# The projections of the HGRN2 heads, the pooling input and the branch gates by Strassen's seven block products

## What is computed

```python
h = rmsnorm(x, gains[2])
z = h @ w_in                       # 1024 x (4*1024 + 512 + 2*1024)
q, fz, iv, og, u, ga, gb = split(z)
k = (1 - lb) * sigmoid(-fz); logf = log(1 - k)
o, s_new = hgrn_chunked(silu(q), k, iv, logf, state)   # 8 heads, chunks of 64
o = o * rsqrt(mean(o * o) + EPS) * a_gnorm
y_a = (o * silu(og)) @ w_a_up
y_b = (scale * groupwise_linear(trailing_mean_w(u) - u)) @ w_b_up   # w = 2, 4, 8, 16
m = sigmoid(ga) * y_a + sigmoid(gb) * y_b
x = x + rmsnorm(m @ w_out, gains[3])
```

## Time and profile before

| | |
|---|---|
| time, median of 3 runs | 2529.26 us (2527.71 to 2529.55) |
| the profiled execution's own time | 2532.01 us |
| its span, first to last instruction | 2530.2 us |
| granted TensorE clock, mean | 0.982 |
| matmuls | 21376 |
| busy share: PE, PEld, DVE, ACT, POOL | 95%, 81%, 51%, 42%, 36% |

### The profile page before, as it was taken

How to read it: one execution, slowest core, us unless ns; L and a number is a source line. 1 busy time by engine, 2 the same in 40 slices (tenths; PEclk the granted TensorE clock), 3 DMA queues, 4 the chain that set the end, 5 groups by cost and what they waited for, 6 DMA issues and landing times.

```text
span 2530.2 us, 54119 instructions
## 1 busy us (share of the span) xinstructions
PE 2401.1 (95%) x21376; PEld 2056.4 (81%) x21376; DVE 1301.3 (51%) x2188; ACT 1060.0 (42%) x1913; POOL 904.3 (36%) x713
## 2 busy tenths in 40 slices
PE   6899999999999999999999999988999999999888
PEld 5688888888888777777878888877888888888776
DVE  7766666300366666666682212268666666000845
ACT  6433333333454444444442332555333334334565
POOL 2577776422212111111221221302777776222110
PEclk9999999999999999999999999999999999999999
DMA  3111112412121011111201112321121112321201
GB/s 124 42 58 50 50 58 63 130 47 68 60 81 37 26 36 36 36 28 36 70 16 38 50 46 87 115 77 35 50 58 55 53 50 79 115 67 48 63 18 69
DMA packets 98195, 147.22 MB, mean 58 GB/s; under 512 B 10160, under 2 KB 43184, under 8 KB 98096
## 3 DMA queue, kind: packets, MB, share of 16 engines
q1 hardware_dynamic: 70352, 121.14, 16.0%
q10 hardware_dynamic: 27744, 24.68, 3.0%
HBM read 131.70 MB, written 14.09 MB: 58 GB/s over the span
## 4 chain that ended last, share of the span: by engine, by line
PE 67%; DVE 21%; issue 8%; ACT 2%; DVEq 1%; POOL 1%; DMA 0%; ACTq 0%; POOLq 0%; SPq 0%
PE bank L687 15%; PE bank L688 15%; PE bank L689 15%; PE bank L718 6%; PE bank L721 6%; PE bank L720 6%; DVE hid L1652 3%; DVE work L1650 3%; DVE hid L1768 2%; DVE hid L1498 1%; PE bank L800 1%; PE bank L833 1%; PE bank L813 1%; DVE ops L1504 1%; DVE hid L1595 1%
## 5 line engine op out<-in xcount | busy, mean ns | idle before, releaser
L597 POOL TENSOR_TENSOR ring<-wtmp,ring 128x512 f16<-128x512 f32 x269 | 339.1, 1263 | 1268.4 <-ACT ring L957 1266.6
L718 PE MATMUL bank<-ops,ring 128*128 128x264 f16 x2240 | 621.2, 277 | 31.5 <-DVE work L1622 22.6
L687 PE MATMUL bank<-ops,ring 128*128 128x264 f16 x2176 | 609.3, 280 | 40.8 <-DVE hid L1689 24.6
L720 PE MATMUL bank<-ops,ring 128*128 128x264 f16 x2240 | 620.8, 277 | 0.0
L721 PE MATMUL bank<-ops,ring 128*128 128x264 f16 x2240 | 620.8, 277 | 0.0
L688 PE MATMUL bank<-ops,ring 128*128 128x264 f16 x2176 | 609.0, 280 | 0.0
L689 PE MATMUL bank<-ops,ring 128*128 128x264 f16 x2176 | 608.6, 280 | 0.0
L687 PE MATMUL bank<-hid,ring 128*128 128x264 f16 x2124 | 589.6, 278 | 1.7 <-DVE hid L2001 1.7
L688 PE MATMUL bank<-hid,ring 128*128 128x264 f16 x2124 | 589.5, 278 | 0.0
L689 PE MATMUL bank<-hid,ring 128*128 128x264 f16 x2124 | 589.4, 278 | 0.0
L610 POOL TENSOR_TENSOR ring<-ring 128x512 f16<-128x512 f32 x240 | 295.1, 1250 | 94.3 <-ACT ring L1008 94.3
(11 more groups left out here) (160 smaller groups left out, 2862.3 us busy)
## 6 DMA issues: line engine op xcount, KB each, us to landing
ring<-weights SPq DMA_DIRECT2D x429, 256.0 KB, 2.7
hid<-xT SPq DMA_DIRECT2D x8, 528.0 KB, 8.3
hid<-out_x ACTq DMA_DIRECT2D x4, 1056.0 KB, 10.9
out_x<-hid ACTq DMA_DIRECT2D x4, 1056.0 KB, 5.4
ops<-xT ACTq DMA_DIRECT2D x3, 1056.0 KB, 9.4
out_x<-ops ACTq DMA_DIRECT2D x3, 1056.0 KB, 5.0
ops<-out_x ACTq DMA_DIRECT2D x3, 1056.0 KB, 8.1
out_x<-ops SPq DMA_DIRECT2D x12, 264.0 KB, 2.2
```

What stands on the lines that cost most here:

```text
L597: nc.gpsimd.tensor_tensor(low(slot), wtmp[:, u % 2, :], high(slot), ALU.subtract).then_inc(unit_ready, 1)
L687: nc.tensor.matmul(out, whi, rhs(t, k, g, 0), start=(k == 0), stop=False)
L718: nc.tensor.matmul(out, whi, xhi, start=(kk == 0 and k != JOINED), stop=False, skip_group_check=True)
L720: nc.tensor.matmul(out, whi, xlo, start=False, stop=False, skip_group_check=True)
```

## The change

The stage `heads` becomes 16 pairs, two per head turn: first q with og, then f with V, and u's four columns at the end in the order w = 16, 8, 4, 2. The gates become eight pairs, one for each m, and beside them runs the plain stage `outs` (up_A and up_B, three units a turn, banks 4 to 7); the pooling's group products are a stage `pools`. These pairs are "chained": they have only banks 0 to 3. Product 2 is added onto product 0 in the same bank, product 4 onto that, product 5 onto that, product 6 onto product 3; ACT copies the bank out after products 0, 2 and 4, and the next product waits for that copy. VectorE adds copy and bank for three of the four blocks, ACT reads the fourth (product 5) itself.

The core of the diff (lines that only pass on new arguments are left out):

```diff
-    "heads": dict(units=8, turns=HEADS, ks=[KD] * 4, kinds="M" * HEADS, banks=4),
-    "gates0": dict(units=8, turns=1, ks=[KD, KD, 1, 1, 1, 1, KD, 4], kinds="M", banks=BANKS),
-    "gates": dict(units=7, turns=7, ks=[KD, KD, KD, 4], kinds="M" * 7, banks=BANKS),
+    "heads": dict(pairs=2 * HEADS, chained=True),
+    "pools": dict(units=1, turns=1, ks=[1] * 4, kinds="M", banks=4, bank0=4),
+    "gates": dict(pairs=KD, chained=True),
+    "outs": dict(units=3, turns=KD, ks=[KD, 4], kinds="M" * KD, banks=4, bank0=4),
...
+CHAIN_BANKS = ((0, 1), (2, 3), (0, 1), (2, 3), (0, 1), (0, 1), (2, 3))
+CHAIN_FRESH = (0, 1, 3)
...
                     with sp.Fori(1, s["pairs"]) as p:
                         load_pair(name, p)
+                        for n in beside:
+                            for u in range(units_of(n)):
+                                load(n, p, u, plan.freed_by(n, p - 1, u))
...
             def head_hooks(h):
                 hh = h - 1
+                return [{
+                    (0, 1): [lambda: keys_and_values(h), lambda: head_transposes(hh, "vT", V)],
+                    (3, 1): [lambda: operands(hh, 1), lambda: head_transposes(hh, "kT", W[3])],
+                    (4, 1): [lambda: operands(hh, 3), lambda: head_scores(hh, "L32", W[0], W[0])],
+                    (6, 1): [lambda: operands(hh, 5), lambda: head_scores(hh, "L16", W[1], W[1]),
+                             lambda: operands(hh, 7), lambda: head_scores(hh, "D16", W[4], W[2])],
+                }, {
+                    (0, 1): [lambda: head_updates(hh, range(4))],
+                    (1, 1): [lambda: head_updates(hh, [4])],
+                    (4, 1): [lambda: operands(hh, 8), lambda: head_outputs(hh)],
+                    (5, 1): [lambda: head_sumsq(hh)],
+                }]
```

The order of ACT in a head turn after the change (p0, p1 are the turn's two pairs; `ahead` takes the high halves for the next turn's first pair):

```diff
+                logf(hh)
+                state_load(hh)
+                chain_copies("heads", p0, 0)
+                if with_norm:
+                    onorm(h - 2, W[4])
+                scale("heads", p1)
+                exps_32(hh)
+                chain_copies("heads", p0, 2)
+                exps_16(hh)
+                to_high("heads", p1, (0, 1), freed0)
+                chain_copies("heads", p0, 4)
+                exps_decay(hh)
+                to_high("heads", p1, (2, 3), freed0)
...
+                    to_high("heads", p1, (4,), freed0)
+                    act.wait_ge(operand_ready, hh * 8 + 8)
...
+                    nc.scalar.activation(Q[:, 0:T], V[:, 0:T], ACT.Silu).then_inc(q_ready, 1)
...
+                    nc.scalar.activation(og, og, ACT.Silu).then_inc(og_ready, 1)
+                    to_high("heads", p1, (5, 6), freed0)
+                chain_copies("heads", p1, 0)
...
+                    scale("heads", h * 2)
...
+                chain_copies("heads", p1, 2)
+                ahead(0, 1)
+                chain_copies("heads", p1, 4)
                 state_store(hh)
+                if not u_turn:
+                    nc.scalar.preload_act_table_set("sigmoid_and_others")
+                ahead(2, 3)
+                osquares(hh)
...
+                    for e in range(2):
+                        b = chained("heads", p1, 5, e)
+                        nc.scalar.activation(gcols(K_, 2 * e + 1), bank[b][:, 0:N], ACT.Sigmoid, scale=-1.0 / WS)\
+                            .then_inc(bank_read[b], 1)
+                    ln_exp_tables()
+                ahead(4, 5, 6)
```

VectorE's order in the same turn (the lines with a minus stood there before; waits left out):

```diff
-                evac_tok(hh, "vT", vtok)
-                if with_norm:
-                    onorm(h - 2)
                 dve.wait_ge(logf_ready, hh + 1)
                 V_.tensor_tensor_scan(GG, smask, W[2], 0.0, ALU.mult, ALU.add).then_inc(cum_ready, 1)
...
+                evac_tok(hh, "vT", vtok)
                 minus_ref(W[0], 64, 31)
+                sums_a("heads", p0, a0)
+                if with_norm:
+                    onorm(h - 2, W[5], W[4])
                 minus_ref(W[1], 32, 15)
                 minus_ref(W[2], 16, 7)
                 operand(W[3], K_, hh, 1)
...
                 evac_scores(hh, "L16", 1)
                 evac_scores(hh, "D16", 2)
+                sums_a("heads", p1, a1)
...
                 V_.tensor_copy(mark[:, 1:2], mark[:, 0:1]).then_inc(chain_ready, 1)
                 if u_turn:
-                    pooling(0)
-                    pooling(1)
+                    pooling(POOL_ORDER[0], p0, 1, 5)
+                    sums_b_odd("heads", p1, b1)
+                    pooling(POOL_ORDER[1], p0, 3, 6)
```

`onorm` loses its product with silu(og): the outputs are multiplied with it when they are read from their banks, and ACT squares them there in four parts. A gate turn of ACT after the change:

```diff
+                def gate_turn(m, dst_a, dst_b, last=False):
+                    prep("outs", m, 0, 1, 2)
...
+                    if not last:
+                        scale("gates", m + 1)
+                    chain_copies("gates", m, 0)
+                    ahead(0, 1)
+                    chain_copies("gates", m, 2)
+                    ahead(2, 3)
+                    chain_copies("gates", m, 4)
+                    ahead(4)
```

Between the first head and the others VectorE and ACT now also make the input sums for the tokens (VectorE's order):

```diff
-            for g in range(1, G):
-                head0_silus(g)
+            t_block(1, (1, 2))
+            head0_silus(1)
+            t_lows(1, 2)
+            t_block(1, (3,))
+            head0_silus(2)
+            t_lows(1, 3, 1)
+            t_block(1, (4,))
+            head0_silus(3)
+            t_lows(1, 4)
             dve.wait_ge(lb_ready, 1)
             decay_keys(0)
```

More of the change, by code:

```diff
@@ L59 @@
 UPS = [("ffn1_up0", "ffn1_up"), ("ffn2_up0", "ffn2_up")]
+BESIDE = {"outs": "gates"}
 PRODUCTS = 7
@@ L176, in __init__ @@
-            for b in range(s["banks"]):
-                uses[b] += self.per(name, b) * s["turns"]
-            unit += s["units"] * s["turns"]
-            ready += s["units"] * s["turns"]
-            plain += s["units"] * s["turns"]
-            used += len(mid_units(name)) * s["turns"]
-            for u in range(s["units"]):
-                loads[self.slot(name, u)] += s["turns"]
-            first = (first + s["units"]) % RING
+            if name in BESIDE:
+                continue
+            group = [name] + [n for n in ORDER if BESIDE.get(n) == name]
@@ L185, in __init__ @@
+            unit += unit_step * (turns - 1)
+            ready += ready_step * (turns - 1)
             if name == "heads":
@@ L665, in take, with turn @@
                     pe.wait_ge(bank_read[b], uses)
-            def turn(name, i, kind, rhs, ready=None, hooks=None):
+            def turn(name, i, kind, rhs, ready=None, hooks=None, order=None):
                 s = STAGES[name]
@@ new lines, in chain_copies, with sums_read @@
+            def chain_copies(name, p, k):
+                for e in range(2):
+                    b = chained(name, p, k, e)
+                    nc.scalar.activation(chain_copy(k, e), bank[b][:, 0:N], ACT.Copy, scale=1.0 / WS)\
+                        .then_inc(bank_read[b], 1)
+            def sums_read(name, p, *ks):
+                for k in ks:
+                    for e in range(2):
+                        b, uses = plan.product(name, p, k, e)
+                        act.wait_ge(bank_read[b], uses + 1)
```

828 lines of the change are left out of this document (484 added, 344 removed).

## The result

The changed kernel takes 2568.13 us (median of 4 runs, 2566.65 to 2570.49) against 2529.41 us for the kernel before (4 runs): a ratio of 1.0155, interval 1.0137 to 1.0172. Slower was forecast, and 2557.4 us.

The account below looks back on a forecast made before the run. TensorE, busy 95% of the span, was taken as the bound. Saving -65.0, steady head turns +43.8, entry +18, last head turn +22.6, into the gates -1.5, gate turns +10.2: +28.1, so 2557.4 us; range 2508 to 2592.

Parts of the forecast that it names:

- kT: Keys' transpose in a head turn: TensorE waits for VectorE's first operand, 23.2 us of chain against 16.4, a 6.9 us hole.
- P4: Last key update, behind product 1 of the second pair: TensorE waits 3.3 us for VectorE's state chain.
- The clock: Behind a hole TensorE's granted clock falls to its lower level: 1.7 to 3.0 us on top, taken as 2.0.
- Entry: Separate first head and turn 1: VectorE's differences and low halves cause waits of 3.6 and about 4 us; net +18.
- Last head turn: Two poolings precede the reading of the output banks, beside the steady turns' waits; net +22.6 us.
- SS: Sums of squares in the last head turn: TensorE waits for output banks behind two poolings, 7.4 us (6.7 to 9.5).
- Into the gates: Turn from the last head into the gates: old waits of 5.8 us and more replaced by smaller ones, net -1.5.
- Gate turns: Product 2 of a gate pair waits 1.7 us for ACT's copy of product 0, six turns, +10.2.
- A: Faster: no hole at the keys' transpose in turns 2 to 8, 7 x 8.9 us less, 2495 us; chance 0.17.
- B: Slower: gate loads queue, a hole of 4 us with its clock, +4.3 in 7 turns, 2587 us; chance 0.13.
- C: VectorE and GpSimd slow each other in the chain before the keys' transpose, 2.3 us x 7, 2574 us; chance 0.12.
- D: Nearly nothing: half of the forecast holes come, 2529 us; chance 0.08.

Follow-up runs that it names:

- experiment 9: The changed kernel with the last key update behind product 3, the head norm behind the third operand, all gate copies first: 2501.92 us, ratio 0.9882.
- experiment 1: The changed kernel with the last key update moved from behind product 1 to behind product 3 of the second pair: 2535.51 us, ratio 1.0007.
- experiment 2: The changed kernel with VectorE's norm of the head before moved from ahead of the first operand to behind the third: 2550.66 us, ratio 1.0057.
- experiment 5: The changed kernel with VectorE's group 1 silus before the first differences and the key decay before the last low halves: 2572.69 us, ratio 1.0146.
- experiment 4: The changed kernel with ACT's gate copies first and high halves 2 to 6 behind the sigmoids: 2549.92, 2549.96 and 2557.13 us, ratio 1.0083.
- experiment 6: The changed kernel with GpSimd's low halves in the head pairs cut to 16 of 512 columns: 2558.00 us, ratio 1.0100.
- experiment 10: experiment 9 with VectorE's sums of product 1, first operand and copies of the keys' transpose made earlier in a head turn: 2511.86 us, ratio 0.9919.
- experiment 12: experiment 10 with D16 scores and key updates one product later, ACT's copy of product 4 first, VectorE's L32 copies and even sums earlier: 2501.68 us.

## Why the prediction was right, by its own steps

**The saving**: right, 576 matmuls; the accounts of both spans close with it.

**Steady turns.** kT: 23.2 us of chain against 16.4 of cover was forecast, 6.9 of hole (the two give 6.8). The changed kernel stands 1.67 at product 3 and 5.01 at kT, together 6.7. ACT's part took 7.1 (898.6 to 905.72) and not 8.0, VectorE's 15.7 (to kT's start at 921.46) and not 15.2, with a stretch by GpSimd of 1.1 in it (2.99 and 1.85 for 2.42 and 1.29). So 22.8 for 23.2, and the cover was 16.1. P4: 3.4 against 3.3, at the place named. The clock: 2.0 a hole was a little dear. In the seven periods TensorE is busy for 410.9 us, and in experiment 9, at full speed, for 387.7 with the same matmuls: 23.2 us for seven holes at kT and seven at P4, 1.7 each. That these holes are the cause, and not the extra work as such, is shown by experiments 1 and 2. The whole was some 7 us too dear over seven periods.

**Table load.** It takes 1.28 us and the next function starts 0.02 us behind it (899.02 to 900.32), as in the earlier trace rows. The drain of 1.38 us that the Trainium skill (ScalarE: Activation LUTs, What ACT_TABLE_LOAD costs) adds is not seen here either.

**Entry.** Holes of 5.8 and 6.3 for the 3.6 and 4 forecast, 1.1 and 3.3 for the 2 and 3.3. The two first were mis-sized: the eight differences took 7.0 us for four where 5.0 stood in the sum, as GpSimd made its first sums beside them. But these are not waits that an order makes, as the sum has them ("stand ahead of"): by experiment 5 VectorE's amount of work is the bound.

**Last head turn: the term that was mis-sized.** The hole at SS was put at 7.4 us, between 6.7 and 9.5, from the poolings' times at the old place (10.9 and 8.8). It is 13.5. The poolings took 13.5 and 11.5. The rows show why, first VectorE's, then GpSimd's of the same 6 us:

```profile
1300.13 1.01 DVE L2141 TENSOR_TENSOR hid<-hid,invc 128x15 f32<-128x15 f32 x1
1301.17 1.19 DVE L2142 TENSOR_TENSOR hid<-hid 128x15 f32<-128x15 f32 x1
...
1303.64 1.03 DVE L2146 SCALAR_TENSOR_TENSOR hid<-hid 128x32 f32<-128x32 f32 x1
```

```profile
1299.47 1.63 POOL L720 TENSOR_TENSOR ring<-ring 128x512 f16<-128x512 f32 x1 [1.83 <-ACT ring L1142]
1301.07 1.26 POOL L724 TENSOR_TENSOR ring<-ring 128x512 f32<-128x512 f32 x1
1303.19 1.43 POOL L720 TENSOR_TENSOR ring<-ring 128x512 f16<-128x512 f32 x1 [0.86 <-ACT ring L1142]
```

An operation on 15 columns takes 1.0 to 1.2 us, and each of the three ends 0.03 to 0.05 us after one of GpSimd's (1301.10, 1302.33, 1304.62). In the run of experiment 4, with the same code up to here but GpSimd a little shifted, two of them were free:

```profile
1297.14 0.18 DVE L2139 TENSOR_TENSOR hid<-hid,invc 128x15 f32<-128x15 f32 x1
1297.35 0.17 DVE L2140 TENSOR_TENSOR hid<-hid 128x15 f32<-128x15 f32 x1
```

and SS waited 9.1 us. So the mechanism of the hole was right; the upper end of its price took GpSimd's presence at the old place as the worst case.

**Into the gates.** Forecast at a net gain of 1.5. It was missed that VectorE's poolings, norm and sums follow each other without a break there, so that every us lost above is also missing here. TensorE stands for 8.7 us between 1332 and 1358 where 6.2 were in the sum. Of the 10.9 us by which the stretch from the last key update to the first join was too cheap, SS explains 6.1, its clock 0.8 (some 5.6 us at the lower level, half of it lost, for the 2.0 in the sum) and these waits 2.5; 1.5 us stay open.

**Gate turns.** 2.2 to 2.8 us at product 2 for the 1.7 forecast, at the place named and with no fall of the clock: 14.3 us in six turns instead of 10.2. Experiment 4 gives them back.

**Rivals.** A (the chain under 16.4 us) did not come about. B (loads queue) did not decide: the wait follows from the copy's place (experiment 4). C (VectorE and GpSimd slow each other) came about by half: two operations of the chain were stretched by 1.1 us a turn together, 8 us in seven turns, for the 16 (2.3 x 7) it was priced at, beside a chain that was otherwise estimated too long. The 14 us of experiment 6 also hold GpSimd's own time. D (half of the holes) did not come about: all the holes named came.

## What to carry to other kernels

Work taken from the busiest engine pays in full only if the other engines' orders are made again for the shorter turn: when a wait appears, look at what stands in front of the late instruction on its engine, work for the next turn first, and at how much later its consumer could be placed (here one hook two products later gave 37 us). Where an engine has no break between two points, an order only deals the holes out anew, and less work is what helps. The same standing time cost less here in three short pieces than in one long one (experiments 9 and 10).

## What the runs showed of the hardware

Two things had not been expected. First, how small an operation of VectorE can be and still wait for GpSimd. The four poolings have 12 operations on 15 or 32 columns. In the changed kernel all 12 took 1.0 to 1.25 us, and wherever GpSimd's rows stand one by one they ended 0.02 to 0.06 us after one of its operations; in the poolings of windows 8 and 16 of the kernel before, with GpSimd mostly idle, five of six took 0.17 to 0.19. The Trainium skill, SBUF — State Buffer, SBUF: two separate sides, calls this an exclusive lock, held for the whole instruction; by that rule the trace agrees. The 0.8 us of the earlier trace rows, which seemed too little for the rule, fit it too: of GpSimd's two operations the first ends at 769.18, 0.92 us after VectorE's began (768.26), and VectorE's ends 1.15 us behind that, 0.14 less than the 1.29 it takes alone. The small ones also end some 0.14 earlier behind GpSimd's than their own 0.17 to 0.19 would have it; why, no run here shows.

Second, equal holes of 3.4 us: of the eight at P4 in the changed kernel six are followed by the lower clock (a mean of 0.50 once and of 0.66 or 0.67 five times over the next 5 us) and two by none. So the price of a single hole of this length can't be read in one place; the mean over seven, 1.7 us, came out of experiment 1, and in traces of equal code it varies. The seven holes of 5.0 us at kT were all followed by the lower level (a mean of 0.50 to 0.60 over the next 5 us), and in experiment 9 the holes of 1.6 to 1.9 were not. In experiment 12 holes of 2.3 to 2.6 were followed by it in about half of the cases (0.68 over the 5 us behind 923.09, 1.00 over the 4 behind 916.92).
